# The second normalisation's two parameter rows are fetched behind the last expert's weights

## What is computed

```python
x1 = _layernorm(DN_ALPHA * x + mix @ w_out, ln1_g, ln1_b)
return _layernorm(DN_ALPHA * x1 + _moe(x1, w_router, b_router, w_gate_up, b_gate_up, w_down, b_down), ln2_g, ln2_b)
# one expert, for the tokens that chose it (top 4 of 32):
gu = xb @ w_gate_up[e] + b_gate_up[e]          # w_gate_up[e]: 1024 x 2048, f32 (8 MB)
hid = (u + 1.0) * g * jax.nn.sigmoid(SWIGLU_ALPHA * g)
return hid @ w_down[e] + b_down[e]             # w_down[e]: 1024 x 1024, f32 (4 MB)
```

## Time and profile before

| | |
|---|---|
| median of 3 runs | 1329.76 us (1328.64 to 1330.32) |
| profiled execution, first to last instruction (span) | 1325.5 us |
| whole time of the profiled execution | not given apart; the median lies 4.3 us above the span |
| PE busy | 1037.9 us, 78% |
| DVE, ACT, POOL busy | 530.9, 228.8, 152.3 us |
| moved by DMA | 499.13 MB, 377 GB/s in the mean |
| chain that ended last: PE, DMA, DVE | 42%, 40%, 6% |

### The profile page before, as it was taken

How to read it: one execution, slowest core, us unless ns; L and a number is a source line. 1 busy time by engine, 2 the same in 40 slices (tenths; PEclk the granted TensorE clock), 3 DMA queues, 4 the chain that set the end, 5 groups by cost and what they waited for, 6 DMA issues and landing times.

```text
span 1325.5 us, 20291 instructions
## 1 busy us (share of the span) xinstructions
PE 1037.9 (78%) x7278; PEld 402.6 (30%) x7279; DVE 530.9 (40%) x953; ACT 228.8 (17%) x504; POOL 152.3 (11%) x136
## 2 busy tenths in 40 slices
PE   7998678977996999855566659975888975868956
PEld 5776343433231333211112113221222321222303
DVE  1699885358432444421112214422414431323324
ACT  1212451222111112100010101210111110101102
POOL 2576722205200000000000000000000000000000
PEclk9999678987997999977677769976989997979978
DMA  9986998998999937899999999799999799999992
GB/s 363 398 313 252 361 363 295 395 365 338 368 422 421 422 128 328 360 422 421 423 422 422 423 422 421 318 421 423 422 422 422 315 424 423 422 421 422 422 422 100
DMA packets 72404, 499.13 MB, mean 377 GB/s; under 512 B 7357, under 2 KB 7930, under 8 KB 19034
## 3 DMA queue, kind: packets, MB, share of 16 engines
q1 hardware_dynamic: 66336, 429.88, 78.9%
q0 software_dynamic: 4688, 67.26, 12.7%
q10 hardware_dynamic: 1354, 1.65, 0.3%
HBM read 496.06 MB, written 2.71 MB: 376 GB/s over the span
## 4 chain that ended last, share of the span: by engine, by line
PE 42%; DMA 40%; DVE 6%; issue 4%; SPq 3%; POOL 3%; ACT 1%; ACTq 0%; DVEq 0%; POOLq 0%
DMA gate_up_w<-in_w_gate_up 27%; PE bank L919 15%; PE bank L968 10%; DMA down_w<-in_w_down 10%; PE bank L575 2%; DVE down_w L1538 2%; PE bank L703 2%; SPq L503 2%; PE bank L980 2%; PE bank L792 2%; DMA ring_b<-in_cache_v,page_row 1%; PE bank L891 1%; PE bank L945 1%; DMA ring_a<-in_cache_k,page_row 1%; POOL ring_b L1473 1%
## 5 line engine op out<-in xcount | busy, mean ns | idle before, releaser
L919 PE MATMUL bank<-gate_up_w,ring_b 128*32 128x512 f32 x3264 | 454.8, 665 | 202.4 <-DMA gate_up_w<-in_w_gate_up 202.1
L1883 DVE TENSOR_TENSOR ring_b<-bank,work 32x512 f32<-32x512 f32 x100 | 68.4, 684 | 484.4 <-ACT work L1260 482.9
L919 PEld LDWEIGHTS bank<-gate_up_w,ring_b 128*32 128x32 f32 x3264 | 90.1, 114 | 449.9 <-DMA gate_up_w<-in_w_gate_up 297.9
L968 PE MATMUL bank<-down_w,ring_b 128*32 128x512 f32 x1632 | 190.5, 600 | 14.9 <-DMA down_w<-in_w_down 14.9
L1480 POOL TENSOR_TENSOR gate_up_w<-gate_up_w,ring_a 128x1024 f32<-128x1024 f32 x1 | 2.3, 2348 | 974.8 <-ACT gate_up_w L1300 974.8
L1260 ACT ACTIVATE work<-bank 32x512 f32<-32x512 f32 x100 | 58.8, 588 | 239.8 <-PE bank L968 238.5
L968 PEld LDWEIGHTS bank<-down_w,ring_b 128*32 128x32 f32 x1632 | 51.6, 112 | 151.2 <-issue 117.7
L1908 DVE TENSOR_SCALAR ring_b<-bank 128x256 f32<-128x256 f32 x51 | 21.6, 424 | 159.8 <-PE bank L919 159.8
L1254 ACT ACTIVATE ring_b<-bank 128x256 f32<-128x256 f32 x51 | 19.5, 383 | 352.7 <-PE bank L945 352.7
L575 PE MATMUL bank<-x_cols,gate_up_w 128*128 128x264 f32 x256 | 62.2, 405 | 0.6 <-ACT x_cols L1098 0.6
L575 PEld LDWEIGHTS bank<-x_cols,gate_up_w 128*128 128x128 f32 x256 | 50.6, 200 | 13.6 <-ACT down_w L1098 2.3
(11 more groups left out here) (370 smaller groups left out, 1031.7 us busy)
## 6 DMA issues: line engine op xcount, KB each, us to landing
gate_up_w<-in_w_gate_up SPq DMA_DIRECT2D x256, 1024.0 KB, 14.8
down_w<-in_w_down SPq DMA_DIRECT2D x128, 1024.0 KB, 11.8
gate_up_w<-in_w_in SPq DMA_DIRECT2D x4, 2048.0 KB, 18.6
gate_up_w<-in_w_out SPq DMA_DIRECT2D x1, 4096.0 KB, 22.2
ring_a<-in_w_in SPq DMA_DIRECT2D x1, 2048.0 KB, 25.7
ring_a<-in_w_mem_kv SPq DMA_DIRECT2D x1, 2048.0 KB, 27.9
down_w<-in_cache_mem_v SPq DMA_DIRECT2D x1, 2048.0 KB, 16.5
x_rows<-in_x_prompt SPq DMA_DIRECT2D x1, 1024.0 KB
```

Of the source, the lines that this page charges most:

```text
L919: last = pe.matmul(p_gu[side][g * SLOTS:(g + 1) * SLOTS, :], xg_t[:, k % 4, k // 4, side * SLOTS:(side + 1) * SLOTS], gate_up_w[:, k, :].r ...
L968: last = pe.matmul(p_down[at_row:at_row + SLOTS, :], hid_t[:, r, k, :], down_rows[:, k, r, h * HALF:(h + 1) * HALF], start=(k == 0), stop= ...
L1883: dve.tensor_tensor(quad_rows[block * SLOTS:(block + 1) * SLOTS, h * HALF:(h + 1) * HALF], bank[1][h * PAIR:h * PAIR + SLOTS, :], down_par ...
```

## The change

The two DMAs of the parameter rows are moved behind the loop over the experts, ahead of `b_down`. The waits that stood in front of them (L470 to L472) are gone: by the place of the new issues all value pages have long been read. All lines below the edit move up by 5, and those behind the new issues by 3.

```diff
@@ -467,11 +467,6 @@
             gu_k = w_gate_up[0].rearrange("e (k p) n -> e p k n", p=PARTS)
             dn_k = w_down[0].rearrange("e (k p r) n -> e p k (r n)", p=PARTS, r=2)
 
-            sp.wait_ge(unit_read, 2 * (NS - 1))
-            for part in range(2):
-                sp.wait_ge(ring_in[(NS - 1) % 2][part], ring_total(NS - 1))
-            sp.dma_start(ln2_gain, ln2_g[0][None, :].broadcast_to([PARTS, D])).then_inc(ln2_in, 16)
-            sp.dma_start(ln2_bias, ln2_b[0][None, :].broadcast_to([PARTS, D])).then_inc(ln2_in, 16)
             sp.wait_ge(pieces_ready, 3)
 
             def load_gate_up(*tiles_k):
@@ -507,6 +502,8 @@
                     sp.dma_start(down_tiles[:, k, :],
                                  dn_k[bass.ds(e, 1), :, k, :].rearrange("a p n -> (a p) n")).then_inc(dn_in[k], 16)
 
+            sp.dma_start(ln2_gain, ln2_g[0][None, :].broadcast_to([PARTS, D])).then_inc(ln2_in, 16)
+            sp.dma_start(ln2_bias, ln2_b[0][None, :].broadcast_to([PARTS, D])).then_inc(ln2_in, 16)
             last_no = sp.value_load(n_blocks[0:1, 1:2], min_val=E - 1, max_val=MAX_BLOCKS - 1)
             sp.wait_ge(gu_used, last_no * KC + 4)
             sp.dma_start(bias_down, b_down[0]).then_inc(down_bias_in, 16)
```

## The result

Median of 6 runs 1334.49 us (1330.26 to 1337.17), beside 1327.97 us for 6 runs of the kernel before (1322.25 to 1330.32). The ratio is 1.0047, 95% interval 1.0025 to 1.0069: 6.2 us slower, 3.3 to 9.2. The profiled execution has a span of 1329.1 us, 3.6 more than the one of before, and took 1330.88 us as a whole.

What follows compares the result with a forecast made beforehand. It took the chain through the last value half's landing to the table as the bound. Terms 6.4 (late pages) + 1.0 (clock) + 0 (end) = +7.4 us on 1329.76 gave 1337.2 us, range 1332.6 to 1339.6.

Steps and rivals of the forecast that it cites:

- the side that had 86%: Sign of the whole change: slower, meaning a time above 1332.4 us, against 11% for same and 3% for faster.
- bound and half of the end rival: Upper end of the range, 1339.6 us: all 3.1 MB pass first (7.5 us), plus half the 3.2 us wait at the end.
- Where the time goes: At SyncE's removed wait: weight tiles issued from 259.1 us fall into the value pages, delaying table and whole expert stream.
- +6.4 us for the last half: Last value half: packet by packet turns let 2.7 MB of weights ahead, so TensorE starts at about 281.6, not 275.25.
- weights' data start about 1.1 us behind the issue ... at 260.2: Start of the early weights' data, as with the parameter rows, when 5.4 MB of value pages are left.
- Clock "+1.0": TensorE's products from the last half on run at low clock 0.50 after longer idle time, adding 1.0 us.
- "0" at the end: Rows behind the last down tiles: `b_down` lands by 1304.9, needed at 1304.98; cost 0, slack 0.1 to some 2 us.
- 3 us of stream: Queue time the two row transfers take up, perhaps 3 us; counted alone, it leaves `b_down` some 2 us to spare.
- Expert 0's weights in time: At the start of expert 0: its weights, last gate tiles issued 7.4 us later, still land in time.
- Turns of whole transfers: Rival at the value pages: engines switch queues per transfer, two down tiles get ahead, 5.0 us, 1335.8 us; chance 12%.
- The pages keep their place: Rival at the value pages: first issued is first served, pages land at 275.2 as before, 1329.8 us; chance 10%.
- the end waits: Rival at the last sums: the row pair takes more than 5.7 us, 3.2 us more, 1340.4 us; chance 8%.

Runs made afterwards that it cites:

- tail_only: Changed kernel with the old waits kept ahead of expert 0's weights, only the parameter rows moved to the end; 1326.82 us, ratio 1.0004 to the kernel before.
- early_only: Changed kernel with the parameter rows and their waits back at the front, behind three early weight tiles; 1333.26 us, ratio 1.0047 to the kernel before.
- tail_3mb: Kernel with only the rows moved and old waits kept, plus an unused 3.1 MB copy between rows and `b_down`; 1334.46 us, ratio 1.0055 to the kernel before.
- one_early: Changed kernel with only down tile 0 issued early, down tile 1 and gate tile 3 held back; 1329.24 us, ratio 1.0011 to the kernel before.
- two_early_4k: Changed kernel with gate tile 3 held back and both early down tiles loaded in 4 KB instead of 8 KB packets; 1331.30 us, ratio 1.0032 to the kernel before.

## Why the prediction was right, and which terms were off

The measured 1334.49 us lies in the range of 1332.6 to 1339.6, on the side that had 86%; the forecast was +7.4 us, the ratio says +6.2. Of the 2.7 us between the forecast of 1337.2 and the median, 1.8 come from the starting value: 1329.76, the median of three runs, against 1327.97 for six. (The range's upper end, "bound and half of the end rival", comes to 1337.2 + 1.1 + 1.6 = 1339.9 when it is added up; nothing hangs on it.)

- *Where the time goes*: right. The wait at L472 had kept expert 0's weights off the value pages; without it the pages are late, and tail_only and early_only split the change into 1.0004 and 1.0047.
- *"+6.4 us for the last half"*: right in mechanism, too large. It measured 5.3 (22.23 less 16.90), and 5.45 to TensorE's start. The turns were as read from the earlier trace rows; mis-sized was the step "weights' data start about 1.1 us behind the issue ... at 260.2". That row was of a queue alone. Beside a page transfer in flight the weights' first packet moved at 263.0, when 4.2 MB of pages were left, of which half, 2.1 MB, at 0.42 MB per us makes 5.0.
- *Clock "+1.0"*: the low stretch during L789 came as forecast, but L832 gave it back in this pair of executions. From the start of the last half to GpSimd's first instruction behind the table it was 37.8 us before (275.25 to 313.05) and 37.5 after (280.70 to 318.20), so -0.3. Measured alike, tail_only and tail_3mb, whose half was not late, took 37.9 and 37.7, and the four others with early tiles 38.5 (one_early), 38.7, 39.3 and 39.9. Over the five kernels with early tiles that is +1.0 in the mean, as forecast, but with a scatter of 2 us and one execution of each: the sign is likely, it is not shown. With the 5.3 of the landing it would make 6.3. A second such place: behind the table the five gather groups from L891 to the second gate product took 4.85 us before (340.92 to 345.77, clock low) and 3.21 after. That is why this pair of executions differs by 5.2 us at the table and by only 3.6 at the end. All runs together give 6.2, with an interval (3.3 to 9.2) that holds both.
- *"0" at the end*: right; 2.9 us of slack were left, more than the 0.1 to 2 that I had worked out. Against the last gate product `b_down` landed 11.1 us later before (1299.3 against 1288.17) and 13.9 after (1305.7 against 1291.78): the pair took 2.8 us of the slack, near the "3 us of stream".
- *Expert 0's weights in time*: right in the changed kernel; the first L916 starts at 317.63, right behind L907, with no wait for a DMA.
- *Rivals.* "Turns of whole transfers" is refuted by equal counts and by two_early_4k, though its 5.0 us was the nearer number, by luck: what made the term smaller than 6.4 was the late start of the weights. "The pages keep their place" fell with the 22.23; "the end waits" needed the 3 MB of tail_3mb to come true.

## What to carry to other kernels

A wait in front of an unimportant transfer may be what keeps the transfers behind it out of a critical one's way: before moving the transfer, list what the wait holds back, and keep the wait if that would run beside something waited for. To estimate what early traffic costs, count packets, not bytes: here the same 2.1 MB cost 4.8 us in 8 KB packets and 2.7 in 4 KB packets. The price is bounded twice, by the early bytes that there are (one tile: 2.5 us) and by the packets that the critical transfer still has to move (two and three tiles: 4.8 and 5.3). A transfer behind the last weights is free only up to the slack between its landing and its use; subtract it from that before moving more there.

## What the runs showed that was not expected

- A queue that joins one at work did not get its first packet through at once: in all five kernels with early tiles the weights' first packets moved 3.4 to 4.4 us after the issue (read in steps of half a microsecond), within half a microsecond of the first small packets (under 512 B) on the page queue. These mark the end of a transfer: there are 47 in 259 to 274 us of the kernel before, where three halves end, 16 for each. On an idle queue it was about 1.1 us. So it looks as if the new queue waited for the end of the transfer in flight; no run varied that end apart from the time since the issue, so this is not shown, and why it would wait stays open.
- TensorE's low stretches move rather than vanish: L835 and its like took 3.47, 5.17, 6.05, 6.11, 6.16 or 6.18 us depending on where they fell. Over the chain from the last half to the table that is a scatter of some 2 us between kernels that differ elsewhere. Later stretches can take it back: in early_only the loop over the experts began 8.9 us later than before (323.49 against 314.55), and the span was only 6.2 us longer. So the price of a change is read from the landing and from many runs, not from one place in one pair of executions.
